# Moving the modulation matmuls of the route stages, and the FFN column transposes, into the attentions of a two-layer diffusion backbone

## What is computed

```python
def modln(x, g, shift, scale):
    return rmsnorm(x, g) * (1 + scale) + shift
...
    for l in range(DEPTH):
        need_ctx = l < DEPTH - 1
        mod = (silu_c @ w_mod[l] + b_mod[l])[:, None, :]
        modc = silu_cc @ w_mod[l] + b_mod[l]
        sh_a, sc_a, gt_a, sh_f, sc_f, gt_f = jnp.split(mod, 6, axis=-1)
        csh_a, csc_a, cgt_a, csh_f, csc_f, cgt_f = jnp.split(modc, 6, axis=-1)
        h = modln(x, g_attn[l], sh_a, sc_a)
        hc = modln(xc, g_attn[l], csh_a, csc_a)
        y, yc = token_mixers(h, hc, w_in[l], conv_w[l], rpb[l], sinks[l], w_branch[l], w_o[l], row, col, need_ctx)
        x = x + gt_a * y
        h2 = modln(x, g_ffn[l], sh_f, sc_f)
        ...
            yt = hier_moe(toks, w_rg[l], b_rg[l], w_re[l], b_re[l], w_e_gate[l], w_e_up[l], w_e_down[l])
            x = x + gt_f * yt[:nl].reshape(x.shape)
```

## Time and profile before

| | us |
|---|---|
| median of 3 runs | 1362.85 |
| lowest, highest | 1360.55, 1365.0 |
| the profiled execution | 1366.03 |
| its span, first to last instruction | 1364.2 |
| PE busy | 1226.1 (90%) |
| mean granted TensorE clock | 0.966 of full speed |

### The profile page before, as it was taken

One profiled execution on the slowest core, in us unless ns is written; L12 is line 12 of the kernel. 1 busy time (PEld: TensorE's weight loads), 2 busy tenths in 40 slices (PEclk: granted clock), 3 DMA queues, 4 the chain that ended last, 5 costly groups with the idle time before them and its releaser, 6 DMA issues.

```text
span 1364.2 us, 22180 instructions
## 1 busy us (share of the span) xinstructions
PE 1226.1 (90%) x8966; PEld 936.5 (69%) x8966; DVE 649.0 (48%) x1503; ACT 438.0 (32%) x1041; POOL 171.6 (13%) x212
## 2 busy tenths in 40 slices
PE   4999888899998989899999789998998868889986
PEld 2788754688887966666666469965998755555652
DVE  1544586464345463422221285667776545233334
ACT  3533366433334350010000364356665510000001
POOL 1810000111011300100000401001111200000001
PEclk9899899999999999999999889999998879999998
DMA  9994145423323279999999985248555859999995
GB/s 353 314 351 151 62 142 192 131 93 93 93 93 124 93 276 417 360 411 414 416 386 373 385 206 155 93 154 264 180 183 188 322 214 419 419 415 415 388 373 185
DMA packets 131831, 351.14 MB, mean 257 GB/s; under 512 B 23054, under 2 KB 84726, under 8 KB 108561
## 3 DMA queue, kind: packets, MB, share of 16 engines
q1 hardware_dynamic: 118144, 317.69, 63.1%
q0 software_dynamic: 12304, 30.37, 6.6%
q10 hardware_dynamic: 1280, 1.66, 0.4%
HBM read 330.53 MB, written 28.86 MB: 263 GB/s over the span
## 4 chain that ended last, share of the span: by engine, by line
PE 80%; DVE 8%; issue 4%; DMA 4%; ACT 2%; POOL 0%; SPq 0%; DVEq 0%; ACTq 0%; POOLq 0%
PE banks L1021 33%; PE banks L1263 16%; PE banks L1277 8%; PE banks L1255 6%; PE banks L1189 4%; PE banks L958 3%; PE banks L1117 2%; PE banks L1132 2%; PE banks L1102 2%; DMA expert_rows<-arena,rows_u 1%; DMA ring<-in_w_in 1%; DMA ring<-in_w_mod 1%; DMA ring<-in_w_e_up 1%; DVE arena L2352 1%; DVE att L2080 1%
## 5 line engine op out<-in xcount | busy, mean ns | idle before, releaser
L1994 DVE TENSOR_TENSOR w_lo_r<-ring,w_hi_r 128x256 fp32r<-128x256 f32 x480 | 222.7, 474 | 241.2 <-ACT w_hi_r L1618 240.1
L1618 ACT ACTIVATE w_hi_r<-ring 128x256 fp32r<-128x256 f32 x480 | 197.4, 416 | 304.6 <-PE banks L1021 254.9
L1263 PE MATMUL banks<-ring,arena 128*64 128x256 f32 x2016 | 233.8, 385 | 28.1 <-issue 11.5
L1021 PE MATMUL banks<-h_hi_r,w_hi_r 128*128 128x512 f32 (+1 forms) x640 | 221.8, 347 | 6.1 <-DVE h_lo_r L1938 4.7
L1263 PEld LDWEIGHTS banks<-ring,arena 128*64 128x64 f32 x2016 | 162.5, 138 | 89.0 <-issue 37.4
L1021 PE MATMUL banks<-h_lo_r,w_hi_r 128*128 128x512 f32 (+1 forms) x640 | 220.2, 344 | 0.0
L1021 PE MATMUL banks<-h_hi_r,w_lo_r 128*128 128x512 f32 (+1 forms) x640 | 220.1, 344 | 0.0
L1021 PEld LDWEIGHTS banks<-h_hi_r,w_hi_r 128*128 128x128 f32 x640 | 122.9, 192 | 22.5 <-ACT arena L1588 4.8
L1021 PEld LDWEIGHTS banks<-h_lo_r,w_hi_r 128*128 128x128 f32 x640 | 123.0, 192 | 13.8
L1021 PEld LDWEIGHTS banks<-h_hi_r,w_lo_r 128*128 128x128 f32 x640 | 122.8, 192 | 13.8
L1277 PE MATMUL banks<-ring,att 128*64 128x512 f32 x424 | 119.3, 604 | 14.1 <-DVE att L2369 7.4
(11 more groups left out here) (269 smaller groups left out, 1726.3 us busy)
## 6 DMA issues: line engine op xcount, KB each, us to landing
ring<-in_w_e_gate SPq DMA_DIRECT2D x64, 1024.0 KB, 8.7
ring<-in_w_e_up SPq DMA_DIRECT2D x62, 1024.0 KB, 9.3
ring<-in_w_e_down SPq DMA_DIRECT2D x53, 1024.0 KB, 9.3
ring<-in_w_mod SPq DMA_DIRECT2D x48, 1024.0 KB, 6.6
ring<-in_w_in SPq DMA_DIRECT2D x38, 1024.0 KB, 5.5
expert_rows<-att POOLq DMA_DIRECT2D x23, 512.0 KB, 20.3
ring<-in_w_o SPq DMA_DIRECT2D x8, 1024.0 KB, 5.1
ring<-in_w_branch SPq DMA_DIRECT2D x8, 640.0 KB, 4.5
```

The costliest lines, as they stand in the source:

```text
L1021: ins = mm(out_ap, a, b, start=k == 0 and p_ == 0, stop=k == KD - 1 and p_ == 2)
L1263: ins = mm(banks[e * CAP:(e + 1) * CAP, bank, 0:DE], x[:, k, e * CAP:(e + 1) * CAP], w[:, k * DE:(k + 1) * DE], start=k == 0, stop=k == KD ...
L1618: fn(w_hi[:, u % AHEAD, :, :], chunk(key)[:, q * KU:(q + 1) * KU, :], ACT.Copy).then_inc(w_hi_ready, 1)
L1994: v.tensor_tensor(w_lo[:, u % AHEAD, :, :], chunk(key)[:, q * KU:(q + 1) * KU, :], w_hi[:, u % AHEAD, :, :].bitcast(F32), ALU.subtract).th ...
```

## The change

- All sections but the first two of layer 0 are now computed in the attentions: six in attention 0 (24 chunks instead of 12), four in attention 1 (16 instead of 12). `MOD_ROUTE` is gone, and with it 12 chunks from route 0 and 4 from route 1.
- The chunks are placed by a table, `MOD_STEP`: in layer 0 one at each of steps 0 to 7, none at 8 and 9, two at 10, one at 11 to 16, two at 17, one at 18 to 23; in layer 1 two, two, one, two, one at steps 0 to 4, none at 5, then two, one, one, two, one, one.
- The FFN sections 4 and 3 come first, and `ffn_columns` runs inside the attention, behind step 8 in layer 0 and step 5 in layer 1, in the bank of the modulation sums. DVE copies the columns out in its next round, ahead of its copy of the transposed probabilities.
- In route 0 three tiles are turned back ahead of the ranks instead of two, and `first_x` waits until all four rounded tiles are there.
- The weight stream has no `w_mod` chunk between the output projection and the experts, so the first six expert weights take their slots during the output projection.

```diff
-MOD_IN = [[(0, 2), (0, 4), (0, 3)], [(1, 2), (1, 4), (1, 3)]]
-MOD_ROUTE = [[(0, 5), (1, 1), (1, 0)], [(1, 5)]]
-MODS = [(0, 1), (0, 0)] + MOD_IN[0] + MOD_ROUTE[0] + MOD_IN[1] + MOD_ROUTE[1]
+MOD_IN = [[(0, 4), (0, 3), (0, 2), (0, 5), (1, 1), (1, 0)], [(1, 4), (1, 3), (1, 2), (1, 5)]]
+MODS = [(0, 1), (0, 0)] + MOD_IN[0] + MOD_IN[1]
...
-        out += [("mod", k, 4 * sec + j) for k, sec in MOD_ROUTE[l] for j in range(4)]
...
+        F_COL = {4: 256, 3: 256 + 2 * KD}
+        F_COL_STEP = [8, 5]
...
-            n = 4 * len(MOD_IN[l])
-            return range(n * s // len(STEPS[l]), n * (s + 1) // len(STEPS[l]))
+            return [q for q, at in enumerate(MOD_STEP[l]) if at == s]
...
                 if b == 7:
-                    sp.wait_ge(f_cols_done, 4)
+                    sp.wait_ge(f_cols_done, 2)
...
                         for i in mod_chunks(l, s - 1):
                             mod(*MOD_IN[l][i // 4], i % 4)
+                        if s - 1 == F_COL_STEP[l]:
+                            ffn_columns(l)
...
-                    if tt >= 2:
-                        pe.wait_ge(th_hi_ready, tt - 1)
+                    if tt == 3:
+                        pe.wait_ge(th_hi_ready, 1)
...
                 if l == 0:
-                    pe.wait_ge(th_hi_ready, 3)
+                    pe.wait_ge(th_hi_ready, 4)
...
-                pe.wait_ge(upd_ready, 4 * QT0[l] + 3 * QT[l])
-                for j2 in range(4):
-                    mod(*MOD_ROUTE[l][0], j2)
                 pe.wait_ge(upd_ready, 4 * (QT0[l] + QT[l]))
-                ffn_columns(l)
-                pe.wait_ge(mod_out, MOD_AT[MOD_ROUTE[l][0]] + 1)
                 turn_h(l)
                 route(l)
                 if l == 0:
-                    turn_rows((0, 1))
-                for k, sec in MOD_ROUTE[l][1:2]:
-                    for j2 in range(4):
-                        mod(k, sec, j2)
+                    turn_rows((0, 1, 2))
                 ranks(l)
                 if l == 0:
-                    turn_rows((2, 3))
-                for k, sec in MOD_ROUTE[l][2:]:
-                    for j2 in range(4):
-                        mod(k, sec, j2)
+                    turn_rows((3,))
                 experts(l)
...
-                mod_add(*MOD_ROUTE[l][0])
                 dve.wait_ge(f_rstd_ready, l + 1)
                 for tt in range(nt):
-                    if tt == nt // 2:
-                        for n, (dst, bank) in enumerate(((f_mul, 6), (f_add, 7))):
-                            dve.wait_ge(f_cols_done, 2 * l + n + 1)
...
+                        if s - 2 == F_COL_STEP[l]:
+                            dve.wait_ge(f_cols_done, l + 1)
+                            for sec, dst in ((4, f_mul), (3, f_add)):
+                                at = F_COL[sec]
+                                v.tensor_copy(dst[:, :, :], banks[:, MOD_BANK, at:at + 2 * KD].rearrange("p (k s) -> p k s", s=2))\
+                                    .then_inc(f_col_ready, 1)
```

More of the change, by code:

```diff
@@ L560, in program @@
         MOD_BANK, O_BANK = 7, 6
-        ROW_BANKS = [(3, 0), (4, 5), (3, 0), (4, 5)]
-        ROUTE_BANK = {(0, 5): 0, (1, 1): 7, (1, 0): 6, (1, 5): 0}
-        def mod_bank(l, sec):
-            return ROUTE_BANK.get((l, sec), MOD_BANK)
+        ROW_BANKS = [(3, 0), (4, 5), (6, 7), (3, 0)]
+        F_COL = {4: 256, 3: 256 + 2 * KD}
+        F_COL_STEP = [8, 5]
+        MOD_STEP = [[0, 1, 2, 3, 4, 5, 6, 7] + [10 + 14 * q // 16 for q in range(16)], [5 * q // 8 for q in range(8)] + [6 + 6 * q // 8 for q in range(8)]]
         def mod_chunks(l, s):
-            n = 4 * len(MOD_IN[l])
-            return range(n * s // len(STEPS[l]), n * (s + 1) // len(STEPS[l]))
+            return [q for q, at in enumerate(MOD_STEP[l]) if at == s]
         E0 = [0, NPAIR]
@@ L951, in mod @@
                     pe.wait_ge(cond_ready, 2)
-                if n and j2 == 0 and (l, sec) not in ROUTE_BANK:
+                if n and j2 == 0:
                     pe.wait_ge(mod_out, n)
+                for m in range(DEPTH):
+                    if j2 == 0 and (l, sec) == MOD_IN[m][2]:
+                        pe.wait_ge(f_col_ready, 2 * (m + 1))
                 landed(pe, ("mod", l, 4 * sec + j2))
@@ L976, in ffn_columns @@
             def ffn_columns(l):
-                for sec, bank in ((4, 6), (3, 7)):
-                    pe.wait_ge(mod_out, MOD_AT[(l, sec)] + 1)
+                for sec in (4, 3):
+                    pe.wait_ge(mod_out, MOD_AT[MOD_IN[l][1]] + 1)
                     for k in range(KD):
+                        at = F_COL[sec] + 2 * k
                         for j in range(4):
-                            ins = mm(banks[32 * j:32 * j + 32, bank, 2 * k:2 * k + 2], modr[:, l, sec, k::KD],
+                            ins = mm(banks[32 * j:32 * j + 32, MOD_BANK, at:at + 2], modr[:, l, sec, k::KD],
                                      ident[:, 32 * j:32 * j + 2], start=True, stop=True)
-                    ins.then_inc(f_cols_done, 1)
+                ins.then_inc(f_cols_done, 1)
             def columns(l, sec):
@@ L1888, in mod_add @@
                 dst = modr[:, l, sec, :]
-                ins = v.tensor_tensor(dst, banks[:, mod_bank(l, sec), 0:CW], dst, ALU.add)
+                ins = v.tensor_tensor(dst, banks[:, MOD_BANK, 0:CW], dst, ALU.add)
                 if sec == 4:
@@ L2544, in _ @@
                 route(l)
-                if l == 0:
-                    mod_add(*MOD_ROUTE[0][1])
                 place(l, False)
                 if l == 0:
-                    rest_rows(0, range(2))
-                    mod_add(*MOD_ROUTE[0][2])
-                    rest_rows(0, range(2, 4))
+                    rest_rows(0, range(4))
                 experts(l)
```

9 lines of the change are left out of this document (3 added, 6 removed).

## The result

The changed kernel takes 1385.5 us (median of 4 runs, 1384.0 to 1392.9) against 1361.7 before (4 runs): a ratio of 1.0182, 95% interval 1.0141 to 1.0223. The prediction had 1370.2 and a range up to 1375.5. The sign was right and the size was a third of what came. The profiled execution took 1383.98 us, the shortest of its four; that of before was the longest of its own, so the profiles show 18 us of the 24.

The account below looks back on a forecast made before the run. PE was taken to set the pace in attention 1, DVE's selection chain in the routes. Attention 0 +6.35, attention 1 +5.4, route 0 0, route 1 -4.4 made 7.35 us slower: 1362.85 to 1370.2 us, range 1360 to 1375.5.

Parts of the forecast that it names:

- The chunks in the attentions: Further chunks, without the columns and the wait for them: 2.95 us in attention 0, 4.15 in attention 1.
- The single adds: Attention 0, steps 12 to 23: three single DVE bias adds of finished sections, +0.3 us together.
- The columns: FFN columns in the attentions delay DVE's copy: +3.4 us at step 8 of attention 0, +1.25 in attention 1.
- Rival 3: Issue gap follows the tiny-matmul burst into an attention or stays in route 1: about 4.3 us more; 0.12 with rival 4.
- rival 4: Loads lag at the end of attention 0, PE waits 2 to 5 us more, 1372 to 1375; 0.12 with rival 3.
- Route 0: Layer 0 route: earlier transposes and dropped waits offset by a cold clock; taken as 0, bounds 5 gained, 3 lost.
- The first gathering: Route 0: its first 5.9 us run at half speed after PE idles, losing 2.95 us.
- warm gate matmuls: First gate matmuls behind route 0 may now find a warm clock, worth half of 3.3 us.
- Route 1: Layer 1 route: issue gap goes, transposes end 4.9 us earlier, cold logit transposes cost 0.5; gain 4.4 us.
- Experts: Both expert stages: earlier loads save no wait, a shift of the start shifts the end; 0.

Follow-up runs that it names:

- Experiment 6: Changed kernel with the columns back in the routes and DVE's adds behind the scaling, all chunks staying in the attentions: 1371.9 us, ratio 1.0058.
- Experiment 3: Changed kernel with the FFN columns back in the route stages, all chunks staying in the attentions: 1380.6 us, ratio 1.0112.
- experiment 1: Changed kernel with DVE's section adds and column copies moved behind the scaling of the probabilities, PE's order untouched: 1375.4 us, ratio 1.0075.
- Experiment 7: Changed kernel with filler matmuls, whose results nothing reads, in the waits of both routes: 1381.3 us, ratio 1.0137.
- experiment 10: Kernel before with three more sections in attention 0, columns in the routes, plus filler matmuls in both routes: 1363.6 us, ratio 1.0002.
- experiment 5: Changed kernel with columns in two halves, the second waiting for the first's copy, and DVE's adds and copies behind the scaling: 1370.0 us, ratio 1.0049.
- experiment 4: Changed kernel with the columns in two halves of 64 matmuls at successive steps: 1388.4 us, ratio 1.0178.
- experiment 12: Changed kernel run once more without any edit, for a second trace: 1386.9 us (one run).
- experiment 2: Changed kernel with another table of steps alone, so that each section ends at an odd step: 1382.4 us, ratio 1.0137.

## Why the prediction was wrong, step by step

- **The chunks in the attentions: right.** Without the columns the sum had 2.95 us for attention 0 and 4.15 for attention 1. Experiment 6 has 3.3 and 4.4.
- **The single adds: the step that failed.** In attention 0 "three single adds, +0.3" priced one at 0.1 us; in attention 1 the sum has no term at all for the adds of the sections that end at steps 4 and 8. Such an add costs the wait for the section's last chunk, with the copy and the scaling queued behind it. Experiment 3 less experiment 6, which differ only in where DVE's adds stand, is 97.6 - 94.2 = 3.4 us in attention 0 and 68.4 - 61.7 = 6.7 in attention 1: 10.1 us. Not all of it is waiting: behind the wait at step 4 of layer 1 the scores and the `attend` run at half clock and take 2.7 us more, which no term of the sum had in an attention either. The prediction worked out this very chain for the columns (chunk or columns behind the scores, DVE's copy behind them) and didn't ask it of the other thing that DVE waits for, though the table of steps shows which sections end at even steps.
- **The columns: mechanism half right, size too small.** Changed kernel less experiment 3 is 4.7 us in attention 0 and 4.1 in attention 1; forecast 3.4 and 1.25. The wait on DVE was there: the pair with the columns took 12.05 us in layer 0 (forecast 11.5), where DVE's copy begins 3.08 us behind the end of the scores, against the 2.45 that I had reckoned, and 0.44 of it is the gap. What was missing is, in layer 1, the gap (2.53 us; 1.25 + 2.53 is 3.8 of the 4.1, and the half clock is there without the columns too) and, in layer 0, the half clock behind the columns. The earlier trace rows had shown half clock right behind the columns of route 1, and the prediction put it down to PE having little to do there. Part of these 8.8 us is DVE's order again: with its work behind the scaling the columns cost 4.0 and 2.3 us (experiment 1 less experiment 6). Rival 3 had the gap, with a chance of 0.12 together with rival 4, and argued against it with the DMA rate; the gap came nevertheless.
- **These make up the miss:** 10.1 + (8.8 - 4.65) + (7.7 - 7.1) = 14.85 us, which is how far the attentions are over their forecast. It must come out even, since the three differences run from one profile to the next (changed, 3, 6, before); in another order of the experiments the shares shift by some 2.5 us between DVE's order and the columns.
- **Route 0: right in its sum.** Forecast 0, measured -0.7. The transposes begin 4.5 us behind the output projection instead of 7.7, that is 3.2 us earlier (forecast 3.25), and lose 2.5 us to the clock (forecast 2.95). Experiment 7 shows the cause: with fillers in the waits the same transposes take 3.76 us instead of 6.33. The first gathering lost 1.3 us and not 2.95, since its second half ran warm. That the sum closes is in part luck: 1.65 us too much for the gathering stood against about as much for the warm gate matmuls, which lie behind this stage.
- **Route 1: right.** Forecast -4.4, measured -5.8; the gap went, and the two cold transposes take 3.65 us together (forecast 3.94).
- **Experts: right.** -0.4 and -0.8 for a forecast of 0. In other runs the stretch from the experts of layer 0 to the projection of layer 1 is 371 to 379 us with the same code, so one profile can't tell a few us there.
- **The range.** Its terms had bounds of 2.5 to 10 us for attention 0 and 2.5 to 7 for attention 1; both measured values lie outside. The bounds were made around the terms that stood in the sum, and the largest cost, the wait with an add, was priced at 0.3 us in one attention and not at all in the other.

## What to carry to other kernels

Price a wait by what is queued behind it on the waiting engine, and ask it of every instruction there that waits for moved work, a 0.42 us add as well as a big one; with rounds that alternate, a table decides by its parity whether the work waited for stands behind a short or a long piece. Work that fills waits may also keep the clock up: when it leaves, count what runs next at half speed, and if fillers replace it, measure one of them first, because what runs over delays the next work (experiments 7 and 10). A pipeline that is bound by latency takes more PE work nearly free (12 chunks for 2.8 us in attention 0), one that PE bounds does not (4 chunks for 4.4 us in attention 1).

## What the runs showed of the hardware that I had not expected

- Tiny matmuls can cost PE its clock, though they keep it busy. In layer 0 the clock fell from 1.00 to 0.50 behind 128 of them, with the gap and without it (experiments 1 and 7), and with two halves of 64 close to each other (experiment 5), where the same steps without them, with more idle time, stayed at 1.00 (experiment 6). It isn't so everywhere. In layer 1 of experiment 5, with scores, an `attend` and transposes between the halves and chunks behind them, the clock held. It held too in route 0 of the kernel before, where chunks stood right ahead of the columns: the 32 transposes behind them took 3.81 us, against 6.33 at a mean clock of 0.57 in the changed kernel.
- A wait of 2.2 us can cost PE its clock as well: in layer 1 of experiment 3, with no columns, the scores and the `attend` behind it took 2.08 and 3.68 us, and in experiments 4 and 12 the transposes right behind it 1.97 instead of 1.09. In layer 0 of experiment 6 a wait of 2.16 us left the clock at 1.00. What decides between the two is open.
- A burst of 128 matmuls of 32 x 2 can make PE stop with nothing to wait for: 0.38 to 2.53 us in the attentions, always behind the 108th in layer 0 and the 126th in layer 1 of the kernels that have such a burst there and no fillers (the changed kernel twice, experiments 1 and 2), and of another length in each execution. The kernel with fillers further on (experiment 7) had no stop at all. The cause is open.
- In the profiles of these kernels the stretch from the experts of layer 0 to the projection of layer 1 took 371 to 379 us, so that smaller effects need several runs or the timeline of the stage itself.
